# A recurrence in eight chunks: the order in which VectorE takes kept products, the next chunk's centring and the level masks

## The reference

```
def step(s, inp):
    r_t, w_t, k_t, v_t, a_t, b_t = inp
    sa = jnp.einsum('bhvk,bhk->bhv', s, a_t)
    s = s * w_t[:, :, None, :] + sa[..., None] * b_t[:, :, None, :] + v_t[..., None] * k_t[:, :, None, :]
    y = jnp.einsum('bhvk,bhk->bhv', s, r_t) if emit else None
    return s, y
```

## Time and profile before

| what | value |
|---|---|
| median of the three runs | 2939.35 us (2938.74 to 2945.32) |
| the profiled execution's own time | 2935.08 us |
| its span | 2933.3 us |
| TensorE (PE) busy | 2817.0 us, 96% of the span |
| VectorE (DVE) busy | 1175.5 us, 40% |
| ScalarE (ACT) busy | 697.1 us, 24% |

### The profile page before, as it was taken

One profiled execution on the slowest core, in us unless ns is written; L12 is line 12 of the kernel. 1 busy time (PEld: TensorE's weight loads), 2 busy tenths in 40 slices (PEclk: granted clock), 3 DMA queues, 4 the chain that ended last, 5 costly groups with the idle time before them and its releaser, 6 DMA issues.

```text
span 2933.3 us, 61839 instructions
## 1 busy us (share of the span) xinstructions
PE 2817.0 (96%) x28070; PEld 1674.7 (57%) x28070; DVE 1175.5 (40%) x2420; ACT 697.1 (24%) x1449; POOL 3.0 (0%) x7
## 2 busy tenths in 40 slices
PE   8999899999999999999988999989999999999997
PEld 3467767445767888874478777873333333333332
DVE  4777565444646444237776454431011010111101
ACT  3345312444322111012454216620000000000000
POOL 0000000000000000000000000000000000000000
PEclk9999999999999999999999999999999999999998
DMA  7100134111332433232000442448999999999995
GB/s 289 58 3 4 34 128 150 44 65 58 115 108 93 144 115 88 79 119 83 30 4 4 152 158 87 151 174 335 416 359 375 408 362 386 392 364 413 364 379 198
DMA packets 188780, 534.44 MB, mean 182 GB/s; under 512 B 6112, under 2 KB 80096, under 8 KB 171104
## 3 DMA queue, kind: packets, MB, share of 16 engines
q1 hardware_dynamic: 187440, 526.21, 47.7%
q0 software_dynamic: 1072, 4.19, 0.4%
HBM read 528.29 MB, written 2.10 MB: 181 GB/s over the span
## 4 chain that ended last, share of the span: by engine, by line
PE 93%; DVE 4%; ACT 1%; issue 1%; DMA 1%; SPq 0%; DVEq 0%; ACTq 0%
PE bank L575 70%; PE bank L714 12%; PE bank L1355 8%; PE bank L833 2%; PE bank L1217 1%; DVE WR L2475 1%; DVE WR L2494 1%; DMA WR<-in_low_first 1%; ACT ar L1652 1%; DVE RS L2603 0%; ACT WR L1652 0%; DVE RS L2368 0%; PE bank L1524 0%; ACT L1652 0%; DVE HT L2280 0%
## 5 line engine op out<-in xcount | busy, mean ns | idle before, releaser
L1652 ACT ACTIVATE ar<-bank 128x256 f32<-128x256 f32 (+2 forms) x360 | 168.5, 471 | 1572.8 <-PE bank L575 1095.4
L575 PE MATMUL bank<-AT,WR 128*128 128x512 f32 (+1 forms) x1408 | 521.4, 520 | 5.7 <-ACT AT L1652 3.7
L575 PE MATMUL bank<-WR,ar 128*32 128x512 f32 (+1 forms) x4464 | 444.5, 555 | 1.6 <-DVE ar L2937 1.6
L575 PE MATMUL bank<-ar 128*32 128x512 f32 (+6 forms) x3990 | 431.2, 510 | 8.7 <-ACT ar L1652 5.9
L575 PEld LDWEIGHTS bank<-AT,WR 128*128 128x128 f32 x1408 | 262.5, 192 | 215.6 <-issue 201.0
L575 PEld LDWEIGHTS bank<-ar 128*32 128x32 f32 (+3 forms) x3990 | 176.3, 124 | 248.5 <-issue 237.4
L575 PEld LDWEIGHTS bank<-WR,ar 128*32 128x32 f32 x4464 | 143.7, 110 | 288.8 <-issue 285.8
L1652 ACT ACTIVATE WR<-bank 128x512 f32<-128x512 f32 (+1 forms) x224 | 122.9, 592 | 217.4 <-PE bank L575 183.7
L575 PE MATMUL bank<-AT,ar 128*32 128x512 f32 (+1 forms) x1456 | 151.8, 562 | 12.1 <-ACT AT L1652 12.1
L2947 DVE TENSOR_TENSOR YB<-YB,bank 128x512 f32<-128x512 f32 x28 | 18.0, 684 | 343.3 <-PE bank L575 343.3
L1652 ACT ACT_TABLE_LOAD x111 | 142.4, 1283 | 13.6 <-DVE ar L2329 7.8
(11 more groups left out here) (367 smaller groups left out, 3295.6 us busy)
## 6 DMA issues: line engine op xcount, KB each, us to landing
WR<-in_moe_w_down SPq DMA_DIRECT2D x27, 2048.0 KB, 15.5
WR<-in_ada_w SPq DMA_DIRECT2D x20, 2048.0 KB, 7.9
ar<-in_moe_w_down SPq DMA_DIRECT2D x20, 2048.0 KB, 14.7
WR<-in_w_in SPq DMA_DIRECT2D x18, 2048.0 KB, 9.1
WR<-in_moe_w_gate SPq DMA_DIRECT2D x18, 2048.0 KB, 17.2
WR<-in_moe_w_up SPq DMA_DIRECT2D x15, 2048.0 KB, 16.2
WR<-in_moe_w_up SPq DMA_DIRECT2D x18, 1536.0 KB, 7.7
WR<-in_moe_w_gate SPq DMA_DIRECT2D x15, 1536.0 KB, 9.0
```

What stands on the lines that cost most here:

```text
L575: return pe.matmul(o, lhsT, rhs, start=first, stop=last)
L1652: return act.activation(out, in_, func, **k)
```

## The change

VectorE's instructions in the second half of a chunk are put in another order. Nothing is added, removed or resized; TensorE's and ScalarE's orders stay. The first two kept products go in front of the centring, the third and fourth in front of `masked(3)`, and the last two in front of `masked(4)`.

```
@@ -2560,18 +2560,18 @@
                     masked(2)
                     if i == 0:
                         v(dve.memset(UV[0:64, :, :, :], 0.0), uv_cleared, wait=False)
+                    kept(i, 0, 2)
                     if i + 2 < NCH:
                         centre(l, i + 2)
-                    kept(i, 0, 2)
                     if i < 4:
                         bonus_keys(l, i)
+                    kept(i, 2, 4)
                     masked(3)
-                    kept(i, 2, 4)
+                    kept(i, 4, 6)
                     if i < NCH - 1:
                         begin_inverse(i + 1)
-                    kept(i, 4, 6)
+                    kept(i, 6, 8)
                     masked(4)
-                    kept(i, 6, 8)
                     if i < NCH - 1:
                         begin_turned(i + 1)
```

## The result

| what | before | after |
|---|---|---|
| median, same chip | 2938.74 us (5 runs, 2935.08 to 2945.32) | 2919.59 us (5 runs, 2914.05 to 2921.82) |
| ratio of the two | | 0.9928 [0.9913, 0.9944] |
| the profiled execution's own time, its span | 2935.08, 2933.3 us | 2919.59, 2917.8 us |

The changed kernel is faster: by 0.72% as the ratio has it, by 19 us (0.65%) between the two medians, and by 15.5 us between the two spans. The time lies in the predicted range, 9.6 us above the point: two thirds of the forecast gain of 29 us arrived.

The account below looks back on a forecast made before the run. TensorE's waits for VectorE were taken as the bound: 11.2 + 5.2 + 2.1 + 13.1 - 0.3 - 2 = 29.3 us less than the median 2939.35, so 2910.0 us. Range 2902 to 2922 us.

Parts of the forecast that it names:

- What bounds: Whole kernel: TensorE is busy 96% of the span; only its waits for VectorE's kept products can go, 36.1 us.
- The 1.40, 0.87 and 1.05 us of a chunk: Level 3, saved per chunk in chunks 4 to 7, 1 to 3 and 0: 11.2, 5.2 and 2.1 us in all.
- almost no waiters left: Sign of being right: on TensorE almost nothing waits any more for L2494, the line of the kept products.
- The second wait, 13.1 us: Behind level 4, in front of L833 in `from_state`: the wait for the last kept pair goes whole, 13.1 us.
- Instruction loads, "I take 2 us": TensorE: removed waits may have hidden gaps at instruction loads; 2 us deducted, between bounds of 0 and 14 us.
- the first rival: TensorE: the waits hid other gaps, 14 us lost instead of 2, gain 17 us, time 2922; chance 0.13.
- the load theory: From the experiments, not the prediction: on TensorE each instruction load risks a gap of its own, wherever it falls.
- The rest of the program: Outside the recurrences: everything is started by TensorE's progress, so it merely shifts and the gain is kept.
- The centring: VectorE's centring moves later, but ScalarE's exponentials keep 0.45 us of slack and its idle time covers more; cost nothing.

Follow-up runs that it names:

- the back half alone: Kernel before with only the last two kept products moved from behind `masked(4)` to in front of it; 2934.43 us, ratio 0.9980 to the kernel before.
- the front half: Changed kernel with kept products 5 to 8 put back where they were, 1 to 4 as changed; 2919.81 us, ratio 0.9932 to the kernel before.

## Why the prediction was right, and where it was too large

**What bounds.** Right. TensorE's waits for L2494 were removed and the time fell. They were counted well too: 18.7 us came back at levels 2 to 4, against 11.2 + 5.2 + 2.1 = 18.5.

**The 1.40, 0.87 and 1.05 us of a chunk.** The distance from the mask of level 2 to that of level 4 fell by 1.48 us in chunk 4, 0.88 in chunk 3 and 1.11 in chunk 0 of layer 0. The mask of level 3 came later as worked out: 4.50 us behind that of level 2 instead of 3.96, where +0.53 was said. Where 0.1 to 0.3 us of waiting for that mask was said, chunk 3 shows 0.10: `inverse_doubled(i, 3)` starts 0.97 us behind `against(i, 4)` instead of 0.87. The 30 waits for masks, 8.1 us in all, are those of weight loads at every level, and before there were 14 for 3.3 us; TensorE's products do not appear in that list. For a kept product they still wait 10 times for 4.1 us, in chunks 0 to 3 alone, 0.41 us in chunk 3. That it waits there follows from the prediction's own times too (251.57 against the end of level 3 at 251.25), though "almost no waiters left" was said.

**The second wait, 13.1 us.** It did go: L833 waits for no kept product. As a change of a wait the step is right. That it shortens the program by as much is wrong: the back half alone gave 5.8 us, and on top of the front half nothing that the times can tell.

**Instruction loads, "I take 2 us".** This is the term that was mis-sized. The gaps put down to issue grew by 11.3 us, near the upper bound of 14 that stood beside it. I took six gaps in 48 loads for the chance that a removed wait uncovers one. But the six were what was left with the waits in place, and say nothing of what the waits covered. With 11.3 in the sum in place of 2 it reads 20.0 us, and the time 2939.35 - 20.0 = 2919.35 us; 2919.59 was measured. That it fits so well is in part luck: in the table of the stretches 29.7 - 11.3 = 18.4 us stand against 17.0 measured. The result thus lies nearer to the first rival (2922), to which 0.13 was given, than to the forecast.

The loads were seen 48 times in this window before and 48 times after:

```profile
q8 instruction: 48, 0.79, 1.6%
```

In both kernels no two of them start less than 3.2 us apart in the recurrences, and most of the smallest distances are 3.4 to 3.5; between the recurrences (400 to 1400 us) they are 17 to 50 us apart. The Trainium skill ("Runtime: NRT & Kernel Launch", section "Instruction fetch mechanics") says that instructions come in 16 KiB blocks of 256 and that the fetch of the next one is mostly hidden. The loads here fit the blocks: each moved 16384 bytes. By count "mostly hidden" holds as well: before, 85 of the 95 loads of both recurrences show no gap, and after it 69 of 96. But by time it does not make the term 0: the gaps are the fetch, as the next lines show, and they cost 15.6 us; the measurement decides.

**The gaps are the fetch.** The traces hold both TensorE's records (products, weight loads, waits) and the times of the loads. Three of the gaps in layer 0 of the changed kernel, us; a block is 256 records:

| TensorE began the block before | the load ran | TensorE went on | gap |
|---|---|---|---|
| 252.74 | 253.27 to 254.51 | 255.91 | 0.51 |
| 296.56 | 297.58 to 298.95 | 300.30 | 1.17 |
| 319.12 | 320.43 to 321.50 | 322.85 | 1.32 |

All 27 gaps of the changed kernel and all 10 of the kernel before stand at the same place of a block: counted in TensorE's records they are multiples of 256 apart, to within one. From gap to gap the number of loads that had landed grows by exactly one for each block passed, so each time TensorE was about to begin the block that had landed last. It went on 1.2 to 1.7 us behind the end of that load. The two waits of 1.75 us in the chunks 0 stand elsewhere in a block, 1.4 and 3.7 us behind a load's end, so they were rightly counted as waits for VectorE. The load of a block starts 0.5 to 2.2 us after TensorE began the block before (the 27 gaps), takes 0.9 to 1.5 us, and the block begins 1.2 us or more behind its end. From the start of one block to the next that makes 3.1 us at the least where there is a gap, while the densest 256 records of layer 0 start within 1.9 us. A wait for VectorE inside the block gives the load that time; without it the same time stands as a gap. That is also why the load theory fails: not every load has the same chance of a gap.

**What is shown and what is not.** Shown: gaps put down to issue take the place of the waits in front of L833, both with and without the front half, and not that of the waits at level 3. Why the waits at level 3 gave no load the time it needed was not worked out. Shown by their place and time: these gaps are TensorE waiting for its next block of instructions. Shown in the profiles, not in the medians: 704 instructions fewer halve them. Not shown: why leaving L942 out saved as much in the medians of the kernel before. The 3.9 us between levels 0 and 2 go with the waits in front of L833 as well: that row of the table reads 129.1 us before and 129.0 with the front half alone, but 132.3 with the back half alone and 133.0 with both; 3.0 of the 3.9 are gaps at block starts.

**The rest of the program.** Right: what follows merely shifted. The stretch between the recurrences was 1106.6 us before and 1108.2 after, the tail 1301.7 and 1300.4; over all the traces of this case they lie between 1106.3 and 1112.6 and between 1298.0 and 1301.7.

**The centring.** Right. The exponentials still start without waiting for it, ScalarE's idle time before the copies of level 3 fell from 1.85 to 0.97 us, before the copy behind L833 from 1.30 to 0.46:

```profile
247.97 1.03 ACT L1652 ACTIVATE ar<-ar 128x256 f32<-128x256 f32 x3
...
251.48 1.09 ACT L1652 ACTIVATE WR<-bank 128x512 f32<-128x512 f32 x2 [0.97 <-PE bank L575]
...
255.45 0.60 ACT L1652 ACTIVATE WR<-bank 128x512 f32<-128x512 f32 x1 [0.46 <-PE bank L833]
```

## What to carry to other kernels

A bank that is filled but not given free costs the engine that fills it: order the consumer so that it gives the bank back in idle time ahead of the critical operation, and count what that does to the critical one. A wait that is removed is worth its length only if nothing else used it: where the waiting engine runs dense streams of short instructions, take the gaps put down to issue that stand in the trace as a floor, not as the risk, and give the term its upper bound. Better, count the engine's records in blocks: a block whose records would run out before the next load has landed uses the waits inside it. Try the two halves of such a change apart: here one half did all that the times can tell.

## What the hardware showed beyond that

Waits on conditions that are already met are not free on TensorE: 32 of them, 16 records in the trace, start 106 ns apart, which is 1.7 us or 53 ns for each wait. In front of level 4 they added only about 0.8 us; in front of L833 the gaps with them are 1.12 to 1.64 us in the changed kernel, and 1.81 where one falls on the start of a block.

The same length of wait had a different worth in two places of one chunk. 18.7 us at levels 2 to 4 came back in full, with gaps unchanged (4.3 to 4.5 us), while 12.7 us in front of L833 came back as 0.7.
